# One comparison for both index tables in each batch of a one-hot gate build, with the row product moved ahead of the batch's own products

## The reference, cut to what matters

```python
top_s, pos = lax.top_k(cand.reshape(TOK_BLOCK, PK_HEADS, TOPK * TOPK), TOPK)
idx = jnp.take_along_axis(cand_idx.reshape(...), pos, axis=-1)      # i * 128 + j
g = jax.nn.softmax(top_s, axis=-1)
a = jax.nn.gelu(jnp.einsum('td,thkd->thk', xb, u[idx]).astype(jnp.float32), approximate=False)
w = (g * a).astype(xb.dtype)
return jnp.einsum('thk,thkd->td', w, v[idx])
```

## Time and profile before

| | us |
|---|---|
| median of 3 runs | 1544.31 |
| lowest and highest | 1543.39, 1545.16 |
| the profiled execution, its own time | 1544.69 |
| its span in the trace | 1542.9 |
| PE busy | 1534.5 (99%) |
| PEld busy | 1364.2 (88%) |
| DVE busy | 1292.7 (84%) |
| POOL busy | 811.3 (53%) |
| ACT busy | 727.4 (47%) |

### The profile page before, as it was taken

How to read it: one execution, slowest core, us unless ns; L and a number is a source line. 1 busy time by engine, 2 the same in 40 slices (tenths; PEclk the granted TensorE clock), 3 DMA queues, 4 the chain that set the end, 5 groups by cost and what they waited for, 6 DMA issues and landing times.

```text
span 1542.9 us, 26071 instructions
## 1 busy us (share of the span) xinstructions
PE 1534.5 (99%) x9474; PEld 1364.2 (88%) x9474; DVE 1292.7 (84%) x2623; ACT 727.4 (47%) x1294; POOL 811.3 (53%) x508
## 2 busy tenths in 40 slices
PE   9999999999999999999999999999999999999998
PEld 9988877888889999999999898989898998888886
DVE  5799675836899999999768888878888898898897
ACT  6333466534335457777643433333343433444435
POOL 3775444434557687666245455556555454344440
PEclk9999999999999999999999999999999999999999
DMA  4322212434334589999889999999999999989993
GB/s 153 98 94 82 68 59 81 159 119 137 92 95 138 178 269 326 358 341 357 261 313 369 365 334 362 345 354 346 350 353 350 348 341 348 347 324 362 355 345 152
DMA packets 158666, 394.47 MB, mean 256 GB/s; under 512 B 20720, under 2 KB 66288, under 8 KB 158448
## 3 DMA queue, kind: packets, MB, share of 16 engines
q1 hardware_dynamic: 59584, 203.14, 36.8%
q0 software_dynamic: 43776, 159.40, 27.8%
q10 hardware_dynamic: 55216, 30.82, 7.0%
HBM read 363.42 MB, written 28.84 MB: 254 GB/s over the span
## 4 chain that ended last, share of the span: by engine, by line
PE 86%; DVE 9%; DMA 3%; ACT 1%; issue 1%; POOL 0%; SPq 0%; ACTq 0%; DVEq 0%; POOLq 0%
PE ps L2379 31%; PE ps L2234 22%; PE ps L1913 7%; PE ps L1976 6%; PE ps L2252 5%; PE ps L2140 3%; DVE rows L1651 3%; DVE hot_w L1797 2%; PE ps L2317 2%; PE ps L1875 2%; PE ps L2153 1%; PE ps L1921 1%; DMA rows<-in_u,gidx_x 1%; DVE hot_l L1793 1%; DMA uraw<-in_uT 1%; DVE hot_l L1798 1%
## 5 line engine op out<-in xcount | busy, mean ns | idle before, releaser
L2234 PE MATMUL ps<-hThi,uwhi 128*128 128x336 f32 x1024 | 318.2, 318 | 0.2 <-ACT act L1078 0.2
L2234 PE MATMUL ps<-hTlo,uwhi 128*128 128x336 f32 x1024 | 317.3, 317 | 0.0
L756 POOL DMA_INDIRECT rows<-in_v,gidx x128 | 177.9, 1390 | 207.6 <-DVE acc L1752 185.9
L756 POOL DMA_INDIRECT rows<-in_u,gidx x128 | 191.6, 1497 | 175.4 <-DVE rows L1745 122.8
L1096 ACT ACTIVATE vwhi<-vraw 128x1024 fp32r<-128x1024 f32 x98 | 104.1, 1062 | 296.9 <-PE ps L2379 287.3
L1035 ACT ACTIVATE uwhi<-uraw 128x1024 fp32r<-128x1024 f32 x128 | 135.5, 1059 | 158.4 <-PE ps L2234 139.1
L2234 PEld LDWEIGHTS ps<-hThi,uwhi 128*128 128x128 f32 x1024 | 192.6, 188 | 1.8 <-issue 0.4
L2234 PEld LDWEIGHTS ps<-hTlo,uwhi 128*128 128x128 f32 x1024 | 192.4, 188 | 1.4
L2379 PE MATMUL ps<-vwhi,awhi 128*128 128x512 f32 x720 | 183.5, 390 | 0.0
L2379 PE MATMUL ps<-vwlo,awhi 128*128 128x512 f32 x720 | 183.4, 390 | 0.0
L2379 PE MATMUL ps<-vwhi,awlo 128*128 128x512 f32 x720 | 182.7, 389 | 0.0
(11 more groups left out here) (389 smaller groups left out, 3147.0 us busy)
## 6 DMA issues: line engine op xcount, KB each, us to landing
uraw<-in_uT SPq DMA_DIRECT2D x128, 512.0 KB, 6.3
vraw<-in_v SPq DMA_DIRECT2D x98, 512.0 KB, 5.8
raw<-in_wstream SPq DMA_DIRECT2D x70, 512.0 KB, 3.5
gmat<-gates_dram SPq DMA_DIRECT2D x64, 384.0 KB, 7.3
gates_dram<-piece ACTq DMA_DIRECT2D x11, 2048.0 KB, 14.9
uraw<-in_v SPq DMA_DIRECT2D x30, 512.0 KB, 6.7
xt<-in_xT SPq DMA_DIRECT2D x8, 264.0 KB, 4.6
acc<-in_x ACTq DMA_DIRECT2D x4, 512.0 KB, 4.4
```

The costliest lines, as they stand in the source:

```text
L756: pool.indirect_dma_start(out=rows[n % SLOTS][:], out_offset=None, in_=u if q < P else v, in_offset=bass.IndirectOffsetOnAxis(ap=gidx[:, q ...
L2234: ins = pe.matmul(ps[:, k, 0:UCOLS], u_weights(a, k, far)[:, c * P:(c + 1) * P], hT[b][:, c, P + EXTRA:TOK], start=i == 0, stop=i == len(U ...
```

## The change

In each of the 38 batches that have row products (0 to 37), one comparison of 128 x 2048 takes the place of the two of 128 x 1024. For this the words of j and i of a batch lie side by side in PSUM (token groups of 8, j then i), and TensorE's transposes write them with that step. The row products of the batch come directly behind the comparison, ahead of the batch's three gate products. In batches 38 to 47 the two comparisons stay apart. No wait is added or taken away, and GpSimd's, ScalarE's, SyncE's and TensorE's programs keep their order and their counts: `extra_before(beside)` in the GpSimd program is as it was.

```diff
-        ji_words, hm_words = (words[k][:, 0:2 * DENSE].rearrange("p (a t) -> p a t", a=2) for k in range(2))
+        ji_words = words[0][:, 0:2 * DENSE].rearrange("p (b a t) -> p b a t", a=2, t=BATCH)
+        hm_words = words[1][:, 0:2 * DENSE].rearrange("p (a t) -> p a t", a=2)
...
-            def hots(batch):
+            every_twice = lanes[:].unsqueeze(1).to_broadcast([P, BATCH, NK, 2])
+
+            def hots(batch, rows_):
...
-                hot_j = chain.mark(dve.tensor_tensor(at_j, every, over_rows(ji_words[:, 0, own]), ALU.is_equal))
-                dve.tensor_tensor(at_i, every, over_rows(ji_words[:, 1, own]), ALU.is_equal)
+                words_ = ji_words[:, first // BATCH]
+                if rows_:
+                    both = words_.rearrange("p a (q r) -> p (a q) r", r=2).unsqueeze(2).to_broadcast([P, BATCH, NK, 2])
+                    hot_j = chain.mark(dve.tensor_tensor(hot_l[:, s].rearrange("p a q n r -> p (a q) n r"), every_twice, both, ALU.is_equal))
+                    for q in rows_:
+                        item_x(q)
+                else:
+                    hot_j = chain.mark(dve.tensor_tensor(at_j, every, over_rows(words_[:, 0]), ALU.is_equal))
+                    dve.tensor_tensor(at_i, every, over_rows(words_[:, 1]), ALU.is_equal)
                 chain.until(hot_j)
...
             for batch in range(NMAIN):
-                hots(batch)
-                for q in range(extra_before(batch), extra_before(batch + 1)):
-                    item_x(q)
+                hots(batch, range(extra_before(batch), extra_before(batch + 1)))
...
+            def indices_of(a):
+
+                return lambda own: ji_words[:, own.start // BATCH:own.stop // BATCH, a]
...
-                    ins = pe.transpose(dst[:, tt * P:(tt + 1) * P], tab[:, tt, :], ident_w[:])
+                    ins = pe.transpose(dst(slice(tt * P, (tt + 1) * P)), tab[:, tt, :], ident_w[:])
...
-                    turned_picks(ji_words[:, 1], tab_ji[:, 1]).then_inc(S["ei_mm"], 1)
+                    turned_picks(indices_of(1), tab_ji[:, 1]).then_inc(S["ei_mm"], 1)
```

More of the change, by code:

```diff
@@ L1784, in _ @@
             every = lanes[:].unsqueeze(1).to_broadcast([P, BATCH // 2, NK, 2])
-            def hots(batch):
+            every_twice = lanes[:].unsqueeze(1).to_broadcast([P, BATCH, NK, 2])
+            def hots(batch, rows_):
                 s, first = batch % 2, batch_tokens(batch)
-                own = slice(first, first + BATCH)
                 if batch == NMAIN:
@@ L1792, in hots @@
                 at_j, at_i = hot_l[:, s, 0], hot_l[:, s, 1]
-                hot_j = chain.mark(dve.tensor_tensor(at_j, every, over_rows(ji_words[:, 0, own]), ALU.is_equal))
-                dve.tensor_tensor(at_i, every, over_rows(ji_words[:, 1, own]), ALU.is_equal)
+                words_ = ji_words[:, first // BATCH]
[7 more added lines that the diff above has]
+                    dve.tensor_tensor(at_i, every, over_rows(words_[:, 1]), ALU.is_equal)
                 chain.until(hot_j)
                 for part in range(2):
-                    dve.tensor_tensor(hot_w[:, s, part], at_j, over_rows(hm_words[:, part, own]), ALU.mult)
+                    dve.tensor_tensor(hot_w[:, s, part], at_j, over_rows(hm_words[:, part, first:first + BATCH]), ALU.mult)
                 dve.tensor_tensor(at_j, at_j, over_rows(lo_words(first, first + BATCH)), ALU.mult).then_inc(S["hot_ok"], 1)
@@ L1811, in _ @@
             for batch in range(NMAIN, NBATCH):
-                hots(batch)
+                hots(batch, ())
             for q in range(SLOTS):
@@ L2272, in added, with weights_of @@
                 return ins
+            def indices_of(a):
+                return lambda own: ji_words[:, own.start // BATCH:own.stop // BATCH, a]
+            def weights_of(part):
+                return lambda own: hm_words[:, part, own]
             def turned_picks(dst, tab):
                 for tt in range(TT - 1):
-                    ins = pe.transpose(dst[:, tt * P:(tt + 1) * P], tab[:, tt, :], ident_w[:])
+                    ins = pe.transpose(dst(slice(tt * P, (tt + 1) * P)), tab[:, tt, :], ident_w[:])
                 return ins
@@ L2296, in _ @@
                         pe.wait_ge(S["tj_ok"], 1)
-                        turned_picks(ji_words[:, 0], tab_ji[:, 0]).then_inc(S["ej_mm"], 1)
+                        turned_picks(indices_of(0), tab_ji[:, 0]).then_inc(S["ej_mm"], 1)
                     if (n, i) == TURN_G:
@@ L2300, in _ @@
                         for part in range(2):
-                            turned_picks(hm_words[:, part], tab_g[:, part])
+                            turned_picks(weights_of(part), tab_g[:, part])
                         for tt in range(TT - 1):
```

## The result

| | before | changed |
|---|---|---|
| median, us | 1544.31 (5 runs, 1543.39 to 1545.16) | 1561.02 (5 runs, 1560.01 to 1562.74) |
| ratio | | 1.0112, 95% interval 1.0101 to 1.0123 |
| span of the profiled execution | 1542.9 | 1558.4 |
| batch loop, from TensorE's first to its last group of small products | 558.5 to 756.5: 198.0 | 556.6 to 772.1: 215.5 |

The change makes the kernel 16.7 us slower; 1562.0 was predicted. In the two profiled executions the loop is 17.5 us longer, and it begins 1.9 us earlier. 17.5 less 1.9 is 15.6, and the spans differ by 15.5 us. So all of the loss lies in the loop.

A forecast was written before the change was run, and what follows sets the result against it. TensorE bounds the kernel, VectorE just behind. Waits of 18.3 us in place of 1.8 give +16.5, followed batch by batch +18; taken +17.7, a span of 1560.6 and median of 1562.0 us, range 1547 to 1573.

The forecast's parts named there:

- Who sets the pace; 1.8 us at most to win: Batch loop: TensorE sets the pace, VectorE just behind; a faster VectorE can give back only 1.8 us.
- Row product and subtraction exclude each other; one-hot operations are not held: VectorE's row product and GpSimd's 2.4 us subtraction shut each other out; one-hots, with one PSUM input, run on.
- Merged comparison 1.15 us: VectorE, 38 batches: one 2048-element comparison takes 1.15 us in place of 1.196, saving 1.9 us in all.
- rival C: Merged comparison is slow, 2.24 us: 1578 us and more; chance 0.08, shared with a stronger clash.
- First batches: Loop start: TensorE waits 1.0, 0.4 and 1.1 us for one-hots at batches 2, 3 and 4, together 2.6.
- The cycle of four: Batches 5 to 37: held row products make four batches take 18.4 us, losing 1.4 a cycle, 11 us over eight.
- The sum: TensorE's loop waits: 2.6 + 11 + 4.6 = 18.3 us in place of 1.8, +16.5; batch by batch +18.
- Rival A: GpSimd stays tied to row products in most blocks, no bad phase: 1542.5 to 1545.5 us; chance 0.13.
- Should the clock fall, far more would be lost: TensorE's clock might fall in its new waits, costing far more; expected to stay at its full level.

The follow-up runs named there:

- e9: Changed kernel with GpSimd's plan for blocks 25 to 55, gathers and subtraction waits together, counted one batch further on: 1542.98 us.
- e8: Kernel before, with the wait of GpSimd's subtractions for row products taken out for blocks 25 to 55: 1566.40 us.
- e3: Changed kernel with the loop's 42 row products taking their second input from PSUM instead of SBUF: 1549.61 us.
- e4: Changed kernel with GpSimd's subtraction of each block waiting for the row products of one batch more: 1565.95 us.

## Why the prediction was right

It was right in sign, size and mechanism (1562.0 against 1561.02). That the number is so close is in part luck: the step from the waits to the sum used 1.8 us where 1.0 was right, and the forecast's +17.7 stands beside a loop that is 17.5 longer, but medians that are 16.7 apart. Step by step:

- *Who sets the pace; 1.8 us at most to win.* Right in kind. The size was wrong by adding the PE and PEld lines: it was 1.0 us, and the best kernel (e9) gets just that back.
- *Row product and subtraction exclude each other; one-hot operations are not held.* Shown, by the 42 row products with a PSUM input, none of them held (1214 to 1222 ns), and for the subtraction by e8 (2.94 us in place of 2.4). The rows of before showed a held row product only. The Trainium skill's rule (SBUF — State Buffer, "Who interferes with whom") agrees with this: with one input in PSUM there is no clash.
- *Merged comparison 1.15 us.* Measured 1.13 from start to start (584.50 to 585.63), two apart take 1.20. So rival C (2.24 us) fell. A batch has five one-hot operations of 0.60 us before the change (two comparisons, three gate products), not four as the account of the batch loop says.
- *First batches.* TensorE's waits at batches 2, 3, 4 were forecast at 1.0, 0.4 and 1.1 us; its starts (560.89, 566.49, 570.81, 576.50, own pace 4.21) give 1.39, 0.11 and 1.48. Sum 3.0 against 2.6.
- *The cycle of four.* Forecast 18.4 us for four batches. From batch 12 (614.52) to batch 16 (633.04) it took 18.52, and from batch 4 to 8 it took 18.51. The forecast loss was 1.4 us for each four batches; the five such stretches without a batch of two row products lost 0.4 to 1.7 us, 1.3 in the mean. That it holds itself was right as well: the 21 held row products go on to the last batch that has any. Its form changes, though: from batch 7 to 16 a hold of about 2 us is followed by one of 0.3, and from batch 19 on mostly two or three holds of 0.8 to 1.5 us follow each other.
- *The sum.* By hand 18.3 us of waits, measured 18.5. Less the 1.8 that was read wrongly that gave +16.5, less 1.0 it is +17.3; followed batch by batch +18, taken +17.7. The loop is 17.5 longer, the median 16.7.
- *A cause that was missed.* Rows that land late. In the changed kernel it is small (3.9 us of waits). It only shows once the holds are gone or GpSimd is tied later, and there it decides (e3, e4). Since holds and late rows hide each other, 11.4 us is what the holds are worth in the presence of the late rows, and not a share that adds up with a second one.
- *Rival A* asked whether GpSimd would stay tied to row products. It was tied in 8 of 29 blocks that waited, and the rival fell. Its condition was the right one: e9 is this rival made true, and ends at 1542.98, inside the 1542.5 to 1545.5 given for it.
- *Should the clock fall, far more would be lost.* It did not fall in the changed kernel. Where it did, a fall cost 1.3 to 1.6 us, four of them 6.2 us (e4).

## What to carry to other kernels

A wait between two engines can be worth its keep without guarding any data, by keeping two operations out of each other's way. Before an operation is moved, look at what the other engines' waits are counted against: the move of one row product by 1.84 us took such a wait out of play in 10 of 18 blocks and cost 1.1%, and a shift of the other engine's plan by the same batch brought it all back. Where a wait is moved later, what is queued behind it moves too (here the gathers), and the whole plan has to go along. And a saving on an engine that is just behind the bottleneck is worth no more than the bottleneck's own waits.

## What the runs showed of the hardware

- A held VectorE operation ends 1.01 us after the GpSimd operation that holds it (587.74 to 588.75), though alone it takes 1.14 (581.83 to 582.97). In the changed kernel all 22 row products that met a subtraction end 1.01 to 1.03 us after it. Whether the first 0.13 us of the work are done while it is held, or the subtraction lets go 0.13 us before its end in the profile, the trace does not tell.
- A held subtraction is late by about what was left of the row product: in e8, beside 2.40 us alone, it takes 2.94 at 581.75 with 0.60 us left, and 3.32 at 667.04 with 0.98 left.
- GpSimd's gathers meet the same row products. One that starts while a row product is at work takes 1.7 to 1.8 us in 21 of 22 cases, one that doesn't takes 0.95; in the changed kernel:

```profile
581.41 0.95 POOL L723 DMA_INDIRECT rows<-in_u,gidx_x  x1
...
587.89 1.76 POOL L723 DMA_INDIRECT rows<-in_u,gidx_x  x1 [0.15 <-issue]
```

  The second was issued 0.86 us before the held row product ended at 588.75, and was over 0.90 us after that. In e3 the twelve gathers that start during a row product with a PSUM input take 0.94 to 0.96 us.
- TensorE's granted clock stayed at its full level (2.4 GHz) in the changed kernel, where the PE row shows waits of up to 1.8 us. In e3, e4 and e8 it fell for short parts of the loop to the lower level, 1.2 GHz, six times in all. Each fall began near the end of a wait for one-hots of 2.1 to 3.3 us, or 0.5 to 0.8 us behind it. What it costs can be read from batch 12, in e4 behind a wait of 2.5 us and in the changed kernel, with TensorE busy throughout in both (e4 first, columns as in the earlier trace rows):

```profile
614.59:620.37 5.78, 5.78 (x43) 5.66 (x43) 5.78 (x8) 2.18 (x2) 2.57 (x3) 0.70 0.90 295
```
```profile
614.52:618.74 4.22, 4.22 (x44) 4.10 (x43) 4.22 (x7) 3.12 (x5) 2.06 (x2) 1.00 1.06 400
```

  The same batch takes 1.56 us more at a mean granted clock of 0.70. The other falls cost 1.3 us (e3, where it began while TensorE still waited) and 1.55 to 1.57 us (e4 three times, e8 once).
